# Moving one scatter behind the next gate/up, and signalling each half of the expert sums as it ends

## What is computed

```python
def _hier_moe(x, w_group, b_group, w_expert, b_expert, w_gate, w_up, w_down):
    ...   # router: one group of 4, the best 2 of its 8 experts, gate weights
    def expert_block(args):
        xb, e = args
        h = jax.nn.silu(xb @ w_gate[e]) * (xb @ w_up[e])
        return h @ w_down[e]
    ...
    y = y[dest] * sgate[:, None].astype(y.dtype)
    out = jax.ops.segment_sum(y, stok, num_segments=n)

for l in range(DEPTH):
    ...
    x = x + mix @ w_out[l]
    x = x + _hier_moe(_rms_norm(x, norm_ffn[l]), ...)
return _rms_norm(x, norm_final)
```

## Time and profile before

| | |
|---|---|
| time, median of 3 | 1280.63 us (1280.54 to 1280.95) |
| the profiled execution: its time, its span | 1280.72 us, 1278.9 us |
| TensorE busy | 1082.8 us, 85% of the span |
| VectorE, ScalarE busy | 348.7 us (27%), 237.5 us (19%) |
| mean granted TensorE clock | 0.917 of full speed |
| read from HBM | 441.58 MB |

### The profile page before, as it was taken

How to read it: one execution, slowest core, us unless ns; L and a number is a source line. 1 busy time by engine, 2 the same in 40 slices (tenths; PEclk the granted TensorE clock), 3 DMA queues, 4 the chain that set the end, 5 groups by cost and what they waited for, 6 DMA issues and landing times.

```text
span 1278.9 us, 18677 instructions
## 1 busy us (share of the span) xinstructions
PE 1082.8 (85%) x7956; PEld 610.2 (48%) x7956; DVE 348.7 (27%) x966; ACT 237.5 (19%) x574; POOL 18.3 (1%) x46
## 2 busy tenths in 40 slices
PE   8999999876878778777799999998777888797876
PEld 4777555433434344434358765553434344334432
DVE  2345562121112111211135454711211121121112
ACT  2234212110111111111112341121111111111211
POOL 1000000000000000000010000000000000000000
PEclk9999999997889898888899999998888888888988
DMA  7774339999999999999993142699999999999993
GB/s 255 256 304 157 132 141 420 426 361 428 425 425 426 423 424 427 426 425 425 408 388 147 63 157 107 236 423 425 426 425 425 424 425 425 424 426 426 425 424 142
DMA packets 62868, 443.88 MB, mean 347 GB/s; under 512 B 10136, under 2 KB 14656, under 8 KB 30016
## 3 DMA queue, kind: packets, MB, share of 16 engines
q1 hardware_dynamic: 61072, 440.94, 84.0%
q10 hardware_dynamic: 1712, 1.71, 0.4%
HBM read 441.58 MB, written 1.06 MB: 346 GB/s over the span
## 4 chain that ended last, share of the span: by engine, by line
PE 49%; DMA 40%; DVE 3%; SPq 3%; issue 2%; ACT 2%; PEld 1%; PEldq 0%; POOL 0%; POOLq 0%; DVEq 0%; ACTq 0%
DMA ring<-in_w_up 38%; PE pv L1489 13%; PE pj L1164 7%; PE tr L1506 5%; PE pj L1170 4%; PE pj L1398 4%; PE pj L1514 3%; PE lg L1514 3%; SPq L375 2%; PE tr L1477 2%; ACT arena L492 1%; PE lg L1199 1%; DMA bias<-bias_lines 1%; DMA ring<-in_w_in 1%; PE pv L1230 1%
## 5 line engine op out<-in xcount | busy, mean ns | idle before, releaser
L1489 PE MATMUL pv<-ring,xT 128*32 128x256 f32 x4096 | 300.6, 458 | 141.4 <-DMA ring<-in_w_up 132.4
L1489 PEld LDWEIGHTS pv<-ring,xT 128*32 128x32 f32 x4096 | 164.8, 131 | 283.4 <-issue 222.9
L1031 DVE TENSOR_SCALAR arena<-arena 128x128 f32<-128x128 f32 x64 | 14.5, 227 | 720.4 <-ACT arena L648 720.1
L1506 PE MATMUL tr<-ring,arena 128*32 128x512 f32 x992 | 125.7, 623 | 18.5 <-issue 18.5
L1514 PE MATMUL pj<-arena 128*128 128x512 f32 x256 | 138.0, 621 | 0.0
L1514 PE MATMUL lg<-arena 128*128 128x512 f32 x256 | 131.4, 595 | 0.0
L492 ACT ACTIVATE arena<-pv 128x256 f32<-128x256 f32 x64 | 24.5, 383 | 556.0 <-PE pv L1489 556.0
L492 ACT ACTIVATE arena<-tr 128x512 f32<-128x512 f32 (+3 forms) x168 | 92.3, 558 | 125.2 <-PE tr L1506 104.9
L1164 PE MATMUL pj<-xT,ring 128*128 128x256 f32 (+1 forms) x480 | 107.9, 381 | 0.6 <-PE pj L1164 0.6
L1164 PEld LDWEIGHTS pj<-xT,ring 128*128 128x128 f32 (+1 forms) x480 | 87.2, 185 | 17.6 <-issue 2.0
L1514 PEld LDWEIGHTS lg<-arena 128*128 128x128 f32 x256 | 50.1, 196 | 64.5 <-issue 64.5
(11 more groups left out here) (199 smaller groups left out, 749.7 us busy)
## 6 DMA issues: line engine op xcount, KB each, us to landing
ring<-in_w_gate SPq DMA_DIRECT2D x64, 2048.0 KB, 29.9
ring<-in_w_up SPq DMA_DIRECT2D x64, 2048.0 KB, 21.6
ring<-in_w_down SPq DMA_DIRECT2D x62, 2048.0 KB, 26.1
ring<-in_w_in SPq DMA_DIRECT2D x10, 2048.0 KB, 19.6
ring<-in_w_out SPq DMA_DIRECT2D x4, 2048.0 KB, 16.9
arena<-in_w_down SPq DMA_DIRECT2D x2, 2048.0 KB, 7.5
ring<-in_w_in SPq DMA_DIRECT2D x2, 1760.0 KB, 12.4
x<-in_x SPq DMA_DIRECT2D x2, 512.0 KB, 4.7
```

Of the source, the lines that this page charges most:

```text
L1031: own.link(v.tensor_scalar(sig, e_neg[:, b], 1.0, None, ALU.add))
L1489: ins = mm(gu_ps[i * CAP:(i + 1) * CAP, :], xg[:, q, j, c:c + CAP], w[:, j, :], start=(j == 0), stop=(j == KD - 1), tile_position=(0, i * ...
L1506: ins = mm(tr[k * CAP:(k + 1) * CAP, half], hid[:, b, k % 2, k // 2, :], down_chunk(flat)[:, k, 512 * half:512 * half + 512], start=True, ...
```

## The change

Three things are changed:

- In each round the scatter of the seventh expert is put behind the products and the turns of the eighth (its wait for the copies of `y` and the freeing of its down slot go with it).
- The last scatter of a layer closes the sums itself and signals `acc_done` for each of its four matmuls; the four matmuls of zeros are gone. VectorE adds half 0 of both tiles, then half 1 of both, each when its own signal has come, and the adds of half 1 signal `x_summed`.
- ScalarE's square sums write their squares over the place of the weighted scatter matrices (`spent`) and no longer over the place that holds `y`.

```diff
-        pgate = take(2 * TOK * QUAD * P).rearrange("p (b t e s) -> p b t e s", b=2, t=TOK, e=QUAD)
+        spent = take(2 * TOK * QUAD * P)
+        pgate = spent.rearrange("p (b t e s) -> p b t e s", b=2, t=TOK, e=QUAD)
...
-                    nc.scalar.activation(zT_flat[:, t * D_MODEL:(t + 1) * D_MODEL], x[:, t, :],
+                    nc.scalar.activation(spent[:, t * D_MODEL:(t + 1) * D_MODEL], x[:, t, :],
                                          ACT.Square, accum_out=ssq[:, t:t + 1]).then_inc(ssq_ready, 1)
...
-                for t in range(TOK):
-                    dve.wait_ge(acc_done, at(l, TOK, t + 1))
-                    for half in range(2):
-                        own.mark(v.tensor_tensor(part(t, half), acc[t][half], part(t, half), ALU.add))
-                    own.after()
-                    dve.sem_inc(x_summed, 1)
+                for half in range(2):
+                    for t in range(TOK):
+                        dve.wait_ge(acc_done, at(l, 2 * TOK, half * TOK + t + 1))
+                        ins = v.tensor_tensor(part(t, half), acc[t][half], part(t, half), ALU.add)
+                        if half == 0:
+                            own.mark(ins)
+                        else:
+                            ins.then_inc(x_summed, 1)
+                own.after()
...
-                def scatter(b, half):
+                def scatter(b, half, last=False):
 
                     for t in range(TOK):
                         ins = mm(acc[t][half], pgT[:, b, t, :], y[:, 512 * half:512 * half + 512],
-                                 start=False, stop=False, skip_group_check=True)
+                                 start=False, stop=last, skip_group_check=True)
+                        if last:
+                            ins.then_inc(acc_done, 1)
                     return ins
...
-                        scatter(e % 2, 0)
+                        scatter(e % 2, 0, m == ROUNDS - 1 and e == BODY - 1)
                         pe.wait_ge(wide_read, at(r, WIDE, y_use(e) + 1))
                         consumed(3 * e + 2)
-                        scatter(e % 2, 1)
+                        scatter(e % 2, 1, m == ROUNDS - 1 and e == BODY - 1)
...
                     down_of(BODY - 2)
-                    add(BODY - 2)
                     products(BODY - 1)
                     turned(BODY - 1)
+                    add(BODY - 2)
                     down_of(BODY - 1)
                     add(BODY - 1)
...
-                for t in range(TOK):
-                    for half in range(2):
-                        ins = mm(acc[t][half], zeros[:, 0:P], zeros[:, P:P + 512], start=False, stop=True,
-                                 skip_group_check=True)
-                    ins.then_inc(acc_done, 1)
```

## The result

The changed kernel took 1271.41 us (median of four runs, 1271.23 to 1272.17) against 1280.79 for the kernel before (four runs, 1280.54 to 1283.81): ratio 0.9924 [0.9908, 0.994], 9.4 us less. The brackets hold the 95% interval of the ratio. The forecast was 1270.5, or 10.1 less. The profiled execution took 1271.42 with a span of 1269.5.

The account below looks back on a forecast made before the run. Weight transfers at 425 GB/s bound the expert stages, TensorE the attention stages. Layer 0 (1.78 + 1.65 + 2.2 = 5.6) and layer 1 (0.67 + 1.68 + 2.11 = 4.5) save 10.1 us from 1280.63: 1270.5, range 1268.8 to 1274.5.

Parts of the forecast that it names:

- When the chunks land: Each layer's last up chunk: landing 21.6 and 21.0 us after issue, at 628.43 and 1251.87; products 0.15 behind.
- The moved scatter: End of each layer's expert stage: scatter covers the 2.31 us wait, saving 1.78 us in layer 0, 0.67 in layer 1.
- The clock: Last down and scatter of each layer: no low clock once the wait is gone, saving 1.65 and 1.68 us.
- The clock rival: Clock falls at the last gate/up or stays low for the last down: one layer 1272.2, both 1273.9; chance 0.20.
- My neighbours: Gate/up groups after waits of similar size: 3.66 us after 2.40, 5.35 after 2.46; 1.8 was put with the full-speed one.
- The end of the sums: Behind each layer's last scatter: no zero matmuls and earlier adds save 2.2 us in layer 0, 2.11 in layer 1.
- The inner rounds and the slots: Six inner round ends earn nothing; the seventh expert's down slot, freed up to about 6.3 us later, costs nothing.
- the 6.3 that I allowed: Seventh expert's down slot: comes free up to about 6.3 us later, from 4.41 + 1.9 of waiting.
- The starved queue: Later down slot starves the weight queue, up to 6.3 us at each of six inner round ends: 1308; chance 0.03.
- My limit of 16: Weight queue: DMA engines run dry only if an issue is more than some 16 us late.
- the hand-over from the second square to the end: End of layer 1: second square to last output product, taken as 2.86 us, as in the kernel before.
- layer 0's share: Layer 0's saving of 5.6 us reaches the end whole, as layer 1's attention stage is paced by TensorE.

Follow-up runs that it names:

- the nine matmuls: Kernel before, in its own order, with nine matmuls of zeros in the wait ahead of each layer's last down product: 1277.25 us, ratio 0.9971.
- the halves: Changed kernel with the first half of the seventh expert's scatter back ahead of the eighth's gate/up, every round: 1271.14 us; timed again, 1270.63.
- the last round alone: Changed kernel with the seventh expert's scatter moved only in each layer's last round, the other rounds in the old order: 1271.64 us, ratio 0.9929.
- the slot freed at the round's end: Changed kernel with the seventh expert's down slot freed behind the eighth's scatter in inner rounds: 1272.48 us, ratio 0.9936.
- the slot freed in the next round: Changed kernel with the seventh expert's down slot freed, in inner rounds, only behind the turns of the next round's first expert: 1280.51 us, ratio 0.9994.

## Why the prediction was right, step by step

- **When the chunks land.** Right: the last up chunk was issued at 607.90 and 1225.84 and landed 21.0 us later both times; the products began at 629.06 (forecast 628.58, with this execution's late start of 0.51 in it), and 0.11 behind the landing in layer 1.
- **The moved scatter, 1.78 and 0.67.** Right. From gate/up to the last down 637.52 - 629.06 = 8.46 and 1255.41 - 1246.95 = 8.46, against 4.41 + 4.10 = 8.51. The wait of 2.31 is covered whole, and what is late next is the chunk: 1.84 and 1.75 us, where I named 1.8 for layer 1.
- **The clock, 1.65 and 1.68.** Right, and shown apart from the move by the nine matmuls. The clock rival (0.20) did not come: no wait of 1.84 or less ahead of a gate/up in this trace was followed by a slow group. But the margin was smaller than I took it for. My neighbours, 2.40 harmless and 2.46 not, are no limit: one wait of 1.92 in the trace of the halves (at 1204.53) was followed by a group of 5.35, and the 2.31 of the round ends is slow too. That 1.84 and 1.75 stayed harmless is in part luck.
- **The end of the sums, 2.2 and 2.11.** Nearly right, 0.1 and 0.2 too much. Layer 0: 645.93 - 642.05 = 3.88 against 3.75, from 5.96: 2.1 saved. Layer 1: 1265.19 - 1259.94 = 5.25 against 5.06, from 7.17: 1.9 saved. Alone the part gave 4.8 in time, a little more than the 4.3 forecast, within its interval.
- **The inner rounds and the slots, nothing.** Right, by the last round alone and by the DMA rate. In the round ends that show it (all but the first of layer 0) the change holds the issue back by 4.5 to 5.7 us (it comes 9.6 to 10.7 behind the one ahead, for 5.1), below the 6.3 that I allowed. The starved queue exists, but further out: 11 to 12 us later than in the kernel before cost nothing and 23 to 24 later cost 1.5. My limit of 16 was on the near side, for it went by landings of 21.0 us, and the chunk that counts takes 29.4.
- **The 0.7 us missing.** 1271.4 and not 1270.5. Between first gate/up and end of span the trace saves 9.91 of the 10.09 forecast; 0.51 more is the late start, which I put down to scatter between executions. Of the 0.18 the hold-up of GpSimd in the last scaling is a part: I had taken the hand-over from the second square to the end as today's 2.86, and it is 1265.19 - 1261.92 = 3.27, since GpSimd's second mean now starts 0.06 behind VectorE's first scaling and takes 1.28, where in the kernel before it took 0.85 (1273.06 to 1273.91). That term was short by 0.4, and the second square's start was a little earlier than I allowed (1.98 for 2.2 behind the pair).
- **One loose reading.** I put the rate in the attention stages at 63 to 236 GB/s; the first three slices of layer 0 have 255 to 304. No term of the sum rests on it, since it is layer 1's attention that layer 0's share has to pass.

## What to carry to other kernels

In a stage that is paced by transfers, a wait of the computing engine is worth taking away only behind the last transfer; find the landing of that one and do the sum from there, for the landing is also what limits the gain. There an idle time of TensorE can cost twice, once as the wait and once as the slow group behind it, so fill it with work that must be done anyway, or failing that with matmuls of zeros. A buffer may be freed late without cost so long as the queue's next issue still comes well before its last one lands; here 13 us before was enough and 1.6 was not.

## What the runs showed of the hardware

- TensorE ran slow after an idle time of 2.31 us with one of 0.75 ahead of it in all eight round ends of the kernel before: the down groups took 2.50 to 3.60 for 1.92, and where the clock was read (the last one) 0.51 was granted, the low level (1.2 GHz). In the kernel after, the 44 gate/up groups behind a wait for their up chunk part cleanly: the 11 with waits of 0.59 to 1.84 took 3.66, the 33 with waits of 2.43 and more took 4.95 to 6.52. Over all fourteen traces the two overlap: the longest harmless wait is 2.44 (the move in the last round alone, at 287.03), the shortest with a slow group behind it 1.92 (the halves, at 1204.53), and the next 2.43. So the length of the wait alone does not decide; what else does, stays open.
- A GpSimd instruction of 0.19 us took 1.28 beside a VectorE instruction of 1.28 that reads two operands of SBUF, and 0.19 without it. In the kernel before the same mean took 0.85 (1273.06 to 1273.91) beside a scaling that ran from 1272.58 to 1273.86. In both cases it ended 0.05 or 0.06 behind VectorE's instruction. The Trainium skill (SBUF — State Buffer, section SBUF: two separate sides) says that such a VectorE instruction and a GpSimd one that reads SBUF take a shared port in turn, each for its whole length; these rows agree. The change moved the mean deeper under the scaling.
- In SyncE's queue a chunk landed 21 to 30 us behind its issue while the DMA engines moved 425 GB/s. A pause of 16.3 us between two issues (the slot freed at the round's end) left the rate as it was; one of 28.6 (the slot freed in the next round) cost 1.5 us.
